# First mixer of a two-block network: upper weight parts one sub further ahead, conv taps spread into the retention, output tiles reordered, some work on ScalarE

## The reference

```python
h = rms_norm(x, mix_norm[l])
rq, rk, rv, rg, mq, mk, mv, ca, cg = split(h @ w_in[l])   # 6 x 64 wide; ca, cg 256
rq, rk = rotary(rq), rotary(rk)                           # 32 pairs of 64
y_ret = (rq @ rk.T * decay) @ rv                          # 6 heads, no softmax
y_ret = silu(rg) * y_ret * rsqrt(mean(y_ret ** 2) + EPS)  # per head
y_moba = softmax(causal(rotary(mq) @ rotary(mk).T / 8)) @ mv   # 6 heads, 256 positions: one block
u = ca * sigmoid(cg)
y = depthwise_conv(u, conv_w, 31 taps, causal) + conv_b
y_conv = silu(group_norm(y) * ln_g + ln_b)                # 4 groups of 64
x = x + concat(y_ret, y_moba, y_conv) @ w_out[l]          # 384 + 384 + 256 = 1024 rows
```

## Time and profile before

| what | us |
|---|---|
| median of 3 runs (lowest, highest) | 2386.27 (2384.91, 2387.98) |
| the profiled execution: time, span | 2384.17, 2382.2 |
| TensorE, VectorE, ScalarE, GpSimd busy | 2280.7, 1561.4, 1140.4, 37.4 |
| first layer: projections, attention, retention and output | 221.7 to 252.4, 252.4 to 303.5, 303.5 to 339.2 |
| second layer: the same | 737.2 to 768.0, 768.0 to 819.0, 819.0 to 854.7 |

### The profile page before, as it was taken

One profiled execution on the slowest core, in us unless ns is written; L12 is line 12 of the kernel. 1 busy time (PEld: TensorE's weight loads), 2 busy tenths in 40 slices (PEclk: granted clock), 3 DMA queues, 4 the chain that ended last, 5 costly groups with the idle time before them and its releaser, 6 DMA issues.

```text
span 2382.2 us, 27252 instructions
## 1 busy us (share of the span) xinstructions
PE 2280.7 (96%) x10956; PEld 1906.1 (80%) x10956; DVE 1561.4 (66%) x2367; ACT 1140.4 (48%) x1755; POOL 37.4 (2%) x40
## 2 busy tenths in 40 slices
PE   7999899999999899999999999899999999998998
PEld 6888778888888878878888877788887788777887
DVE  4546765555557669967985545689689955447565
ACT  4445454444444454544445555544444455554443
POOL 0000000000000000000000000000000000000000
PEclk9999999999999999999999999999999999999999
DMA  7554435555554348866974433588779854334663
GB/s 257 182 198 138 127 125 199 190 189 183 177 188 133 122 149 301 305 216 216 314 274 143 142 124 106 169 274 303 240 254 309 284 161 138 123 106 162 215 215 124
DMA packets 250386, 462.94 MB, mean 194 GB/s; under 512 B 9542, under 2 KB 55536, under 8 KB 250132
## 3 DMA queue, kind: packets, MB, share of 16 engines
q1 hardware_dynamic: 250020, 461.04, 57.8%
q10 hardware_dynamic: 240, 0.16, 0.0%
HBM read 460.12 MB, written 1.05 MB: 194 GB/s over the span
## 4 chain that ended last, share of the span: by engine, by line
PE 78%; DVE 16%; ACT 4%; issue 2%; POOL 0%; DMA 0%; ACTq 0%; DVEq 0%; POOLq 0%
PE ps L1605 15%; PE ps L1608 15%; PE ps L1606 15%; PE s L1608 6%; PE s L1605 6%; PE s L1606 6%; DVE wl L2155 5%; DVE acc L2163 4%; PE ps L1580 3%; DVE cacc L2335 2%; PE s L1715 2%; PE ps L1735 1%; ACT wh L1900 1%; PE ps L1621 1%; PE ps L1620 1%
## 5 line engine op out<-in xcount | busy, mean ns | idle before, releaser
L2155 DVE TENSOR_TENSOR wl<-raw,wh 128x1024 fp32r<-128x1024 f32 (+3 forms) x742 | 855.3, 1177 | 383.2 <-ACT wh L1900 378.3
L1900 ACT ACTIVATE wh<-raw 128x1024 fp32r<-128x1024 f32 (+1 forms) x748 | 743.2, 1020 | 325.2 <-PE ps L1608 216.2
L1605 PE MATMUL ps<-wh,xh 128*128 128x512 f32 (+3 forms) x1632 | 628.9, 385 | 11.5 <-DVE wl L2155 11.4
L1608 PE MATMUL ps<-wh,xl 128*128 128x512 f32 (+3 forms) x1632 | 613.5, 376 | 0.0
L1606 PE MATMUL ps<-wl,xh 128*128 128x512 f32 (+3 forms) x1632 | 612.6, 375 | 0.0
L1605 PEld LDWEIGHTS ps<-wh,xh 128*128 128x128 f32 x1632 | 308.7, 189 | 77.4 <-DVE wl L2155 17.4
L1608 PEld LDWEIGHTS ps<-wh,xl 128*128 128x128 f32 x1632 | 308.5, 189 | 47.8
L1606 PEld LDWEIGHTS ps<-wl,xh 128*128 128x128 f32 x1632 | 309.1, 189 | 44.7
L2163 DVE SCALAR_TENSOR_TENSOR acc<-raw,condT,acc 128x512 f32<-128x512 f32 x252 | 189.4, 751 | 7.7
L1605 PE MATMUL s<-wh,xh 128*128 128x512 f32 x384 | 150.3, 391 | 1.8 <-DVE wl L2155 1.8
L1608 PE MATMUL s<-wh,xl 128*128 128x512 f32 x384 | 149.6, 389 | 0.0
(11 more groups left out here) (329 smaller groups left out, 2696.0 us busy)
## 6 DMA issues: line engine op xcount, KB each, us to landing
raw<-in_ffn_w_in SPq DMA_DIRECT2D x80, 1024.0 KB, 5.2
raw<-in_ada_w SPq DMA_DIRECT2D x72, 1024.0 KB, 5.2
raw<-in_ffn_wg SPq DMA_DIRECT2D x40, 1024.0 KB, 5.3
raw<-in_ffn_wu SPq DMA_DIRECT2D x40, 1024.0 KB, 5.3
raw<-in_ffn_wd SPq DMA_DIRECT2D x40, 1024.0 KB, 5.2
raw<-in_ffn_w_out SPq DMA_DIRECT2D x40, 1024.0 KB, 5.5
raw<-in_mix_w_in SPq DMA_DIRECT2D x28, 1024.0 KB, 5.1
raw<-in_w_in SPq DMA_DIRECT2D x28, 768.0 KB, 4.4
```

The costliest lines, as they stand in the source:

```text
L1605: e.matmul(o, X[0](kk, t), hi, start=kk == 0, stop=False)
L1608: ins = e.matmul(o, X[1](kk, t), hi, start=False, stop=kk == K - 1)
L1900: ins = self.e.activation(m.wh[j % NH][:, 0:n], m.raw[u % NR][:, k0 * w:k0 * w + n], ACT.Copy)
L2155: ins = self.e.tensor_tensor(m.wl[j % NH][:, 0:n], m.raw[u % NR][:, k0 * w:k0 * w + n], hi, ALU.subtract)
```

## The change

- `ahead` makes upper parts up to LA = 4 subs ahead and lets one lower part lag, so lower parts stay three ahead. Before a residual sum (`into_x`) nothing lags and the depth is as before. This holds in the whole kernel.
- Posts may have their own lag: conv input 2 subs, retention's queries and keys 4, others 3.
- One tap behind each fill in projections and attention; the rest (three a step), the conv's turn and its norm steps (two a step) go into the retention's steps as `conv_work`.
- Tile pairs of the output product: (3,4), (5,0), (6,7), (1,2) for (3,4), (5,6), (7,0), (1,2); the first four subs use the first two pairs only; the conv pair is turned after them, directly ahead of the last retention pair.
- The squares of the retention norm and of the conv norm, and the scaling of ungated attention values (also in the second block), are issued on ScalarE.

```diff
-LA = 3
+LA = 4
-TAPS = (3, 2, 1)
-WO_TILES = ((3, 4), (5, 6), (7, 0), (1, 2))
-WO_SEQ = ((0, 0), (0, 1), (1, 0), (2, 0), (1, 1), (3, 0), (2, 1), (3, 1))
+WO_TILES = ((3, 4), (5, 0), (6, 7), (1, 2))
+WO_SEQ = ((0, 0), (0, 1), (1, 0), (1, 1), (2, 0), (3, 0), (2, 1), (3, 1))
...
-    def ahead(self, n=LA):
+    def ahead(self, n=LA, behind=1):
         while self.wsub < self.taken + n and self.made < len(self.k.w.subs):
             self.make()
+            if len(self.later) > behind:
+                self.lower()
+        while len(self.later) > behind:
+            self.lower()
...
             self.later.append((j, u, k0, nk, un["w"], last))
-            if not later:
-                self.lower()
...
-        self.ahead(LA if plain else NH - len(two))
+        self.ahead(3 if plain else NH - len(two), 0)
...
+        st.valued, st.inverse = self.new(self.s.prod, "value"), self.new(self.s.vec, "inverse")
+        st.done = self.new(self.s.act if st.gate is None else self.s.vec, "out")
...
-                self.posts.append((self.taken, post))
+                self.post(post, LAG if n[0] == "m" else LAG + 1)
...
         while not {"mq", "mk", "mv"} <= set(rdy):
             self.fill()
-            taps(TAPS[0] if len(self.jobs) > 5 else TAPS[1])
+            taps(1)
 
         def step_fill():
-            n = len(self.posts)
             self.fill()
-            taps(0 if len(self.posts) > n else TAPS[2])
+            taps(1)
...
-        taps(31)
...
+        def conv_work():
+            if conv["k"] < 31:
+                taps(3)
+            elif "turned" not in conv:
+                conv["turned"] = True
+                b = self.next_t()
+                self.conv_turn(l, b, tok)
+                self.free[b] = (s.act, ("yc", l))
+            else:
+                conv_steps(2)
...
-            if i == 1:
-                conv_steps(8)
-            after = [[ymoba, self.rt_free] + tok, [ymoba, normed], [yret.get(0), normed], [yret.get(1), yret.get(2)]][i]
+            after = [[ymoba, self.rt_free], [ymoba, yret.get(0)], [normed], [yret.get(1), yret.get(2)] + tok][i]
...
-            elif wo_n[0] < 2 or (wo_n[0] == 2 and 0 in yret):
-                if wo_n[0]:
-                    turn_wo(wo_n[0])
+            elif wo_n[0] < 4:
+                if wo_n[0] == 1 and 1 not in ytok:
+                    turn_wo(1)
                 wo_sub()
...
+            if h > 2 and h % 2:
+                j = (h - 3) // 2
+                yret[j] = (s.vec, ("yret", l, j))
+                self.ret_square(l, j)
             step()
             if h > 2 and h % 2:
                 while "rg" not in rdy:
                     self.fill()
-                j = (h - 3) // 2
-                yret[j] = (s.vec, ("yret", l, j))
                 self.ret_norm(l, j, read[-1], rdy["rg"][0])
-            if h == 0:
-                b = self.next_t()
-                self.conv_turn(l, b, tok)
-                self.free[b] = (s.act, ("yc", l))
-            else:
-                conv_steps(2)
+            conv_work()
+        while nconv[0] < 8:
+            conv_work()
         while wo_n[0] < 4:
-            if wo_n[0] < 3:
-                step()
-            else:
-                wo_sub()
+            step()
+        turn_wo(2)
         turn_wo(3)
...
+    def value_part(self, st):
+        m = self.m
+        if st.gate is not None:
+            return
+        self.wait_ge(st.inverse, st.valued)
+        for i, sgm in enumerate(st.segs):
+            o = st.i * 128 + 64 * sgm["t"]
+            ins = self.e.activation(m.ym[:, sgm["t"], st.col:st.col + 64], m.ps[7][:, o:o + 64], ACT.Copy,
+                                    scale=st.sm[:, 6 + i:7 + i])
+        self.then_inc(ins, st.done)
...
+        if i == 2:
+            self.wait_ge((self.s.vec, ("cn", l, 1)))
+            self.then_inc(self.e.activation(m.yc2[:, :, :], m.yc[:, :, :], ACT.Square), (self.s.act, ("convsq", l)))
...
+    def ret_square(self, l, j):
+        m, c = self.m, slice(128 * j, 128 * j + 128)
+        self.wait_ge((self.s.act, ("reto", l, 2 * j + 1)))
+        self.then_inc(self.e.activation(m.ym[:, :, c], m.zt[1][:, :, c], ACT.Square), (self.s.act, ("retsq", l, j)))
...
-        self.wait_ge(self.own(e.tensor_tensor(q, y, y, ALU.mult), "squared"))
+        self.wait_ge((s.act, ("retsq", l, j)))
```

More of the change, by code:

```diff
@@ L434, in take @@
             self.make()
+        while j not in self.lo_at:
+            self.lower()
         hs, nk, un = self.sub_of[j]
@@ L437, in take, with make @@
         return j, hs, nk, un["w"]
-    def ahead(self, n=LA):
+    def ahead(self, n=LA, behind=1):
         while self.wsub < self.taken + n and self.made < len(self.k.w.subs):
             self.make()
-    def make(self, later=False):
+            if len(self.later) > behind:
+                self.lower()
+        while len(self.later) > behind:
+            self.lower()
+    def make(self):
         subs = self.k.w.subs
@@ L702, in skewed @@
         while self.wsub < self.taken + 4:
-            self.make(later=True)
+            self.make()
         v0 = self.turn_scaled(s, 0, (self.next_t(), self.next_t()))
@@ L957, in values @@
     def values(self, st):
-        st.valued = self.new(self.s.prod, "value")
-        st.done = self.new(self.s.vec, "out")
+        st.valued, st.inverse = self.new(self.s.prod, "value"), self.new(self.s.vec, "inverse")
+        st.done = self.new(self.s.act if st.gate is None else self.s.vec, "out")
         self.value_part(st)
@@ L975, in pair_step, with post @@
         return st
+    def post(self, f, lag=LAG):
+        self.posts.append((self.taken + lag, f))
     def job(self, label, done):
@@ L990, in fill @@
             j["k"] += n
-        while self.posts and (not self.jobs or self.posts[0][0] + LAG <= self.taken):
+        while self.posts and (not self.jobs or self.posts[0][0] <= self.taken):
             self.posts.pop(0)[1]()
@@ L1090, in post @@
                 conv["tok"] = [tp, tp]
-            self.posts.append((self.taken, post))
+            self.post(post, LAG - 1)
         def q_done(n, zi, rot):
@@ L1215, in mix1 @@
                     [(wo_b[0], 8), (wo_b[1], 4)], td=last[0])
+    def ret_square(self, l, j):
+        pass
     def tap(self, l, k, c, after, done):
@@ L1279, in post @@
                 self.pt_free = [tk, tk]
-            self.posts.append((self.taken, post))
+            self.post(post)
         rope2 = (m.cos2, m.sin2, 8, cst)
@@ L2279, in value_part @@
         self.wait_ge(st.segs[-1]["exp"])
-        ins = e.reciprocal(r, st.sm[:, 4 + t0:4 + t0 + n])
-        self.wait_ge(self.own(ins, "inverse"))
-        if n == 1:
-            self.wait_ge(st.valued)
-            ins = e.tensor_scalar(m.ym[:, t0, c], m.ps[7][:, at + 64 * t0:at + 64 * t0 + 64], r, None, ALU.mult)
-        elif st.gate is None:
-            self.wait_ge(st.valued)
-            ins = e.tensor_tensor(m.ym[:, :, c], m.ps[7][:, at:at + 128].rearrange("p (t e) -> p t e", t=2),
-                                  r.unsqueeze(2).broadcast_to([P, 2, 64]), ALU.mult)
-        else:
-            f = m.small[:, 80:82]
-            self.wait_ge(self.own(e.tensor_tensor(f, st.gate, r, ALU.mult), "weight"), st.before(), st.valued)
-            for t in range(2):
-                y = m.ym[:, t, c]
-                ins = e.scalar_tensor_tensor(out=y, in0=m.ps[7][:, at + 64 * t:at + 64 * t + 64], scalar=f[:, t:t + 1], in1=y,
-                                             op0=ALU.mult, op1=ALU.add)
+        self.then_inc(e.reciprocal(r, st.sm[:, 4 + t0:4 + t0 + n]), st.inverse)
+        if st.gate is None:
+            return
+        f = m.small[:, 80:82]
+        self.wait_ge(st.inverse)
+        self.wait_ge(self.own(e.tensor_tensor(f, st.gate, r, ALU.mult), "weight"), st.before(), st.valued)
+        for t in range(2):
+            y = m.ym[:, t, c]
+            ins = e.scalar_tensor_tensor(out=y, in0=m.ps[7][:, at + 64 * t:at + 64 * t + 64], scalar=f[:, t:t + 1], in1=y,
+                                         op0=ALU.mult, op1=ALU.add)
         self.then_inc(ins, st.done)
@@ L2354, in conv_norm @@
             ins = e.tensor_reduce(three(s0), y4, AX.X, ALU.add)
-        else:
-            self.wait_ge((self.s.vec, ("cn", l, i - 1)))
+        elif i != 2:
+            self.wait_ge((self.s.vec, ("cn", l, i - 1)) if i != 3 else None)
         if i == 1:
@@ L2360, in conv_norm @@
         elif i == 2:
-            ins = e.tensor_tensor(z4, y4, y4, ALU.mult)
+            return
         elif i == 3:
+            self.wait_ge((self.s.act, ("convsq", l)))
             self.wait_ge(self.own(e.tensor_reduce(three(s1), z4, AX.X, ALU.add), "var"))
@@ L2385, in ret_norm @@
         sm0, sm1, sm2 = (m.small[:, 64 + 12 * i + 4 * j:68 + 12 * i + 4 * j] for i in range(3))
-        self.wait_ge(read)
-        self.wait_ge(self.own(e.tensor_tensor(q, y, y, ALU.mult), "squared"))
+        self.wait_ge((s.act, ("retsq", l, j)))
```

2 lines of the change are left out of this document (1 added, 1 removed).

## The result

The changed kernel takes 2433.60 us (median of 4 runs, 2431.69 to 2433.91), the kernel before 2385.7 beside it: ratio 1.0198, 95% interval 1.018 to 1.0215. It is slower by 2.0%; I had forecast 2369 and put 0.08 on slower.

What follows compares the result with a forecast made beforehand. Only TensorE's idle or slow time could be won. Per mixer -3.5 - 8.4 + 0.4 + 2.2 = -9.3, both -18.6; plus 1.5 outside: 2384.2 to 2367.1, and 2.1 to the median: 2369 us, range 2359 to 2382.

Steps and rivals of the forecast that it cites:

- The step that failed: Stretches with condition vectors (`ada`): accumulations now precede the previous sub's lower part; from -2 to +5 us, taken as 0.
- The recorded rival: At `ada` units TensorE wants lower parts earlier than VectorE gives them: 1.6 us a place, slower from 14 places; chance 0.08.
- Projections and attention: First block's mixers, per mixer: projections 27.2 us against 30.7, minus 3.5; attention 42.7 against 51.1, minus 8.4.
- the replay: Attention's queues replayed in the new order: TensorE waits about 0.9 us for queries, 0.9 keys, 0.8 last value product.
- Retention: Retention stage of each first-block mixer: output sub five starts at 36.1 us against 35.7, plus 0.4.
- Two terms: Retention: TensorE's list takes 30.7 us; VectorE's, 31.4, ends at 33.1, Silu at 34.1, so TensorE waits 3.4.
- The half-speed stretch behind this wait: End of retention, behind TensorE's conv tile wait: about 4 us at half speed, plus 2.2 us per mixer.
- The conv tile is in time: Rival in retention: VectorE loses less than charged, so the 3.4 and 2.2 us go, giving 2358; chance 0.12.
- Values on ScalarE: Second block's attention: ungated values scaled on ScalarE come about 0.2 us later before forget matrices, plus 1.5 us in all.
- the squares: Retention and conv norm squares on ScalarE: cost nothing; 0.4 us if the last norm's cover goes.

Runs made afterwards that it cites:

- SP's late release alone: Lower parts first, with only the weight unit's load put back behind the `ada` load and its accumulations, as the change had it: 2429.98 us.
- lower parts first: The changed kernel, but at every `ada` unit the lagging lower part is made, and its buffer released, before the four accumulations: 2371.84 us.
- SP's order alone: The changed kernel with only SP's queue altered: `ada` load and bias row issued after the lagging lower part's load: 2411.31 us.
- light ones: Each `ada` load fetches one 256 KB block of four: changed kernel 2410.3 us, lower parts first 2371.4, the same with late release 2398.4.
- the old mixer: The kernel before with the look-ahead of four, one lagging lower part, and lower parts first ahead of accumulations, nothing else of the change: 2370.71 us.
- the last two kernels: Lower parts first with eight taps moved from retention into attention, 2370.76 us; then that with last norm's tile turned later, two taps moved into projections, 2366.96.
- the last kernel: Lower parts first with taps moved from retention into attention, two then into projections, and the last norm's tile turned one output sub later: 2366.96 us.

## Why the prediction was wrong

**The step that failed** is the one outside the mixers: "In the stretches with condition vectors ... VectorE's sum is the same; ScalarE's copies come earlier, the accumulations too. From -2 ... to +5 ...; I take 0", with "SP's queue is untouched" before it. I asked of the lagging lower part who waits for its result, and found TensorE with room. I did not ask who waits for its *end as a reader*: the buffer it gives back, and SP, which must issue that load in order. Measured: 60.6 us there, and SP's late release alone makes 58.1 of the 61.8 us that lower parts first win back. I quoted the row that should have warned me: DMA share 0.91 at 312 GB/s. I read it for VectorE's 98% alone. A release 3.0 us late (four accumulations), at 72 units, would cost 72 x 3.0 = 216 us if each were exposed and nothing caught up (an estimate). Over two thirds of that is caught up, and still +5 could not be the upper end.

The Trainium skill (DMA: Bandwidth & Descriptors, section on the anatomy of one DMA) says that DMA engines do not wait on semaphores, and that every such wait is spent on the issuing sequencer. By that rule a waiting `ada` load holds whatever stands behind it; the 308.1 us of SP's waits and the 22.3 us won by SP's order alone agree.

**The recorded rival** of the slower side had the right place and the right sign, but another mechanism: 1.6 us a place by VectorE's order. By the table that order is worth 3.6 us with full loads, which is within the spread of single runs, and 11.9 with light ones.

**Projections and attention** (-3.5, -8.4) came out: 26.8 and 42.7 us, no wait for `wl`, none over 1 us for `ptT` (in the whole kernel 2.8 us, longest 0.7), clock 1.00. The waits of the replay are there too: 0.5 and 0.7 us for the turned queries and keys (I had 0.9 each), 0.7 for the scaled value (0.8). With the old taps and posts the look-ahead alone cuts the wait of 4.0 us to 1.0; in the first layer a stretch at half speed remains there (clock 0.93 over 47.1 us), in the second it doesn't (1.00 over 44.0).

**Retention** was mis-sized: +0.4 was 41.3 - 35.7 = +5.6. Two terms were too small. TensorE came to the conv tile 33.8 us into the stage and not at 30.7: it waited 1.2 us for ScalarE's copy of `yc`, and it ran at half speed at the stage's start, which I did not have at all. And I counted VectorE's list as if its inputs were there. After, it idles at four places that I did not have:

```profile
309.05 0.42 DVE L2420 TENSOR_TENSOR rg<-rg,zt 128x256 f32<-128x256 f32 x1 [1.99 <-ACT rg L2025]
314.14 0.43 DVE L2407 TENSOR_TENSOR pt<-s,cst 128x256 f32<-128x256 f32 x1 [1.02 <-PE s L1793]
316.20 0.69 DVE L2329 TENSOR_TENSOR y1l<-ps,y1h 128x512 fp32r<-128x512 f32 x1 [1.44 <-ACT y1h L2013]
...
323.81 0.69 DVE L2396 TENSOR_TENSOR yc<-yc,small 128x512 f32<-128x512 f32 x1 [1.60 <-POOL small L2584]
```

Together 6.0 us; the conv's Silu is ready at 38.7 us into the stage and not at 34.1. TensorE meets it thus:

```profile
329.94 1.97 PE L1595 MATMUL ps<-cst,ym 128*128 128x128 f32 x8 [4.93 <-ACT ym L2056]
332.47 0.80 PE L1620 MATMUL ps<-wh,y1h 128*128 128x512 f32 x1 [0.56 <-DVE y1l L2329]
```

The half-speed stretch behind this wait, which I took for 2.2 us, came and was longer. These windows show it, and before it the one at the stage's start:

```profile
292.00:296.00 4.00, 4.00 (x16) 3.99 (x16) 3.00 (x7) 1.55 (x2) 0.00 (x0) 0.57 0.00 0
330.00:336.00 6.00, 5.44 (x16) 4.32 (x17) 3.65 (x4) 2.14 (x3) 0.00 (x0) 0.50 0.12 15
```

With its edges, between 329.8 and 336.6 us, the second is 6.8 us at half speed, which costs 3.4; 4.1 us of it lie behind the stage's end at 332.50. The first is 3.4 us at half speed and costs 1.7. I had asked only about stretches behind a long wait; the longest waits in the ten microseconds before this one were 0.74 and 0.67 us. The Trainium skill (TensorE: Matmul & The Clock Gate, HAM clock gate) says that half rate is the default, which idleness brings back; the trace agrees for the stretch behind 4.93 us. What brought the other one stays open.

**"The conv tile is in time"** did not happen by itself, but the last two kernels made it true, and its price was near: they won 5.6 and 3.7 us a mixer over lower parts first, where that rival gave 5.6. **Values on ScalarE** cost nothing measurable in the second block (I had 1.5); the squares were not tried by themselves.

**The two layers differ by the clock.** With the look-ahead confined to it, the first layer's mixer gains 2.1 us and the second 6.9. Its windows say why:

```profile
178.43:342.57 164.14, 153.97 (x792) 135.18 (x791) 107.34 (x218) 83.02 (x153) 6.47 (x5) 0.95 0.43 135
691.90:851.25 159.35, 149.20 (x792) 131.22 (x791) 107.27 (x218) 83.02 (x153) 6.47 (x5) 0.98 0.44 139
```

TensorE idles for 10.2 us in both; the 4.8 us between them are its busy time, at a clock of 0.95 and 0.98. It is the same in every run whose mixers are given here: the idle time of the two mixers agrees within 0.1 us (12.3 before, 10.2 after, 8.8 with the old mixer, 7.2 in the last kernel), and what differs is half-speed stretches that come in one layer and not in the other. So a gain of a few us in a mixer is better read from both layers, and from TensorE's idle time, than from one length.

## What to carry to other kernels

When an instruction is moved back in its queue, follow two things from it: who waits for its result, and what its end gives back. A buffer returned late delays the next load, and an in-order issuing queue passes the delay on to loads of other buffers; here, in stretches whose mean DMA share was 0.75 to 0.83, 58 us of a bound of 216 were not made up. And a stage's estimate as "the sum of one engine's list" is a lower bound: go through the inputs of each instruction once, above all where a small one goes through GpSimd and back.

## What the runs showed of the hardware that was not expected

Three loads, 2 MB in all, issued within 1.6 us after a pause landed 7.70 us after the last issue, where the page's median from issue to landing for that load is 5.3; I read this as the price of loads that come in a bunch, from one place. Between the holes the queues moved up to 422 GB/s in a slice of 0.5 us, above the 296 of the 20 us around it. And the clock didn't follow the longest wait alone: with TensorE nine tenths busy the attention kept 1.00, while behind its last waits of 0.74 and 0.67 us the clock fell at about 292.2 for 3.4 us in the first layer and not in the second, and the wait of 4.93 us was followed by 6.8 us at half speed.
